# A two-layer hybrid decoder trunk on one core: two small experts in one slot, and the final norm inside the last slot

## The reference, cut to what matters

```python
def _rmsnorm(x, g):
    y = x * lax.rsqrt(jnp.mean(x * x, axis=-1, keepdims=True) + EPS)
    return y * g

def expert_block(xb, e):                       # D = D_FF = 1024
    hb = xb @ w1[e] + b1[e]                    # w1: 1024 x 2048
    x_glu = jnp.minimum(hb[:, :D_FF], 7.0)
    x_lin = jnp.clip(hb[:, D_FF:], -7.0, 7.0)
    return (x_glu * sigmoid(1.702 * x_glu) * (x_lin + 1.0)) @ w2[e] + b2[e]

h = h + sum over a token's 4 experts of gate * expert_block(norm(h), e)
out = _rmsnorm(h, norm_final)
```

## Time and profile before

| | us |
|---|---|
| median of three runs | 2594.08 |
| lowest and highest run | 2588.51 and 2594.45 |
| the profiled execution, its own time | 2597.89 |
| its span, from the first to the last instruction | 2596.1 |
| TensorE busy, all phases | 2418.1 |
| first expert matmul to last | 890.3 to 2551.5 |
| mean granted TensorE clock | 0.968 |

### The profile page before, as it was taken

One profiled execution on the slowest core, in us unless ns is written; L12 is line 12 of the kernel. 1 busy time (PEld: TensorE's weight loads), 2 busy tenths in 40 slices (PEclk: granted clock), 3 DMA queues, 4 the chain that ended last, 5 costly groups with the idle time before them and its releaser, 6 DMA issues. The chain is left out here.

```text
span 2596.1 us, 29106 instructions
## 1 busy us (share of the span) xinstructions
PE 2418.1 (93%) x11256; PEld 1585.8 (61%) x11257; DVE 632.6 (24%) x1536; ACT 365.9 (14%) x825; POOL 431.4 (17%) x998
## 2 busy tenths in 40 slices
PE   7899988989896699999999999999999999999993
PEld 3445556434443485968769678587686686684441
DVE  2031165222435521212122122121121221211111
ACT  3001054011311001010110101100101111101111
POOL 3806882020010101010000100000001001000002
PEclk9999988999997899999999999999999999999996
DMA  8604111610005558586787887878878888989854
GB/s 196 162 0 65 44 16 53 163 60 0 1 1 209 196 180 243 202 265 215 270 273 249 265 272 264 268 258 273 278 256 281 287 284 281 299 282 314 283 173 146
DMA packets 373344, 508.03 MB, mean 196 GB/s; under 512 B 49032, under 2 KB 234632, under 8 KB 373205
## 3 DMA queue, kind: packets, MB, share of 16 engines
q1 hardware_dynamic: 360872, 469.43, 55.0%
q0 software_dynamic: 11008, 35.89, 6.2%
q10 hardware_dynamic: 1324, 0.83, 0.1%
HBM read 469.39 MB, written 38.77 MB: 196 GB/s over the span
## 5 line engine op out<-in xcount | busy, mean ns | idle before, releaser
L2069 PE MATMUL ps<-xT,we 128*128 128x160 f32 (+9 forms) x3584 | 516.7, 307 | 1.4 <-ACT xT L2316 1.4
L2069 PEld LDWEIGHTS ps<-xT,we 128*128 128x128 f32 x3584 | 508.5, 190 | 15.1 <-issue 8.0
L2011 PE MATMUL ps<-we,xT 128*128 128x512 f32 x1152 | 506.8, 594 | 0.0
L2011 PEld LDWEIGHTS ps<-we,xT 128*128 128x128 f32 x1152 | 213.8, 190 | 258.5 <-issue 258.5
L2083 PE MATMUL ps<-actT,we 128*128 128x160 f32 (+9 forms) x1792 | 261.1, 307 | 0.0
L2083 PEld LDWEIGHTS ps<-actT,we 128*128 128x128 f32 x1792 | 253.4, 190 | 5.6 <-DVE outT L2230 2.1
L2035 PE MATMUL ps<-we,actT 128*128 128x512 f32 x576 | 255.1, 596 | 0.7 <-ACT actT L2347 0.7
L1906 POOL DMA_INDIRECT acc_dram<-orow,sx x46 | 70.9, 1542 | 779.0 <-ACT orow L2327 487.2
L2339 ACT ACTIVATE sg<-glu 128x512 f32<-128x512 f32 (+9 forms) x92 | 49.8, 541 | 1040.7 <-DVE glu L2185 549.6
L2035 PEld LDWEIGHTS ps<-we,actT 128*128 128x128 f32 x576 | 106.6, 190 | 135.1 <-issue 134.2
L795 PE MATMUL ps<-xnT,wa 128*128 128x512 f32 x384 | 168.9, 601 | 7.6 <-DMA wa<-in_w_in 7.6
(11 more groups left out here) (333 smaller groups left out, 2143.8 us busy)
## 6 DMA issues: line engine op xcount, KB each, us to landing
we<-in_w SPq DMA_DIRECT2D x384, 1024.0 KB, 5.9
wa<-in_w_in SPq DMA_DIRECT2D x4, 2048.0 KB, 12.9
xrow<-in_x SPq DMA_DIRECT2D x32, 128.0 KB, 7.4
wa<-in_w_xkv SPq DMA_DIRECT2D x2, 2048.0 KB, 10.2
h<-in_x SPq DMA_DIRECT2D x4, 1024.0 KB
acc_dram<-h SPq DMA_DIRECT2D x1, 4096.0 KB
fin<-acc_dram SPq DMA_DIRECT2D x8, 512.0 KB, 8.9
out<-fout SPq DMA_DIRECT2D x32, 128.0 KB, 2.4
```

What stands on the lines that cost most here:

```text
L2011: last = nc.tensor.matmul(m.ps[:, 2 * part + c, :], m.xT[:, 4 * half + k, 0:P], view[:, k, :], start=False, stop=(half == 1 and k == 3), s ...
L2069: last = nc.tensor.matmul(bank[:, part * WIN:part * WIN + W], view[:, k, (j % 2) * P:(j % 2 + 1) * P], m.xT[:, k, 0:W], start=(k == 0), st ...
```

## The change

The ranks 30 and 31 get a width of 64 and one slot for both, the second; there are 31 slots. A slot's pieces now come expert by expert in turn, so the joined slot has 24. Each of its matmuls is done twice, once for each expert: 64 columns of tokens stationary, PSUM partitions 0 to 63 for the one and 64 to 127 for the other, same bank. Its bias matmuls have three rows, with the rows that select the half in `sel`. It has two gathers and two scatters of 64 rows, the second scatter waiting for the first. Three VectorE instructions are added before the first slot.

The phase of the final norm is gone. In the last slot, once the scatter of the slot ahead has landed, SP loads four blocks, waits for them, and loads four more; POOL gathers the last slot's own rows from `acc_dram` into `tail`. ACT squares four blocks between the slot's two sigmoids and four after its last copy for the second layer. POOL makes the roots, VectorE scales in place, SP stores. VectorE then adds the last slot's result from PSUM to `tail`; ACT, POOL and VectorE norm it, and POOL stores it by index over the rows already stored. The last slot's own scatter is done only if tokens spilled, and then the whole norm is repeated.

The diff, cut to its core:

```diff
-RANK_WIDTH = (256, 224, 200, 168, 164, 164, 160, 160, 160, 156, 144, 136, 136, 132) + (P,) * 18
-RANK = tuple(r for i in range(14) for r in (i, 31 - i)) + (17, 16, 15, 14)
+RANK_WIDTH = (256, 224, 200, 168, 164, 164, 160, 160, 160, 156, 144, 136, 136, 132) + (P,) * 16 + (64, 64)
+SLOTS = ((0,), (30, 31)) + tuple((r,) for i in range(1, 14) for r in (i, 30 - i)) + ((16,), (15,), (14,))
...
 def piece_used(eng, n):
-        s, i = divmod(n, PIECES)
+        s = max(t for t in range(NS) if PIECE0[t] <= n)
+        i = (n - PIECE0[s]) // len(SLOTS[s])
...
     def _(sp):
...
+            if s == 0:
+                sp.dma_start(m.gfin[:], a.norm_final.rearrange("(a n) -> a n", a=1).to_broadcast([P, D])).then_inc(gfin_in, 16)
+                sp.dma_start(m.high[ST:P], m.gate_l[0:ST]).then_inc(high_in, 16)
+                for r in range(4):
+                    sp.dma_start(m.sel[32 * r:32 * r + 1, 0:ST], ...)
+                    sp.dma_start(m.sel[32 * r + 2:32 * r + 3, ST:P], ...)
+                for r in (2, 3):
+                    sp.dma_start(m.sel[32 * r + 1:32 * r + 2, :], ...)
...
+        q = out_tile(LAST - 1, 0)
+        sp.wait_ge(scattered[q % 2], 16 * (q // 2 + 1))
+        piece_used(sp, PIECE0[LAST] - 1)
+        for b in range(NB):
+            if b % 2 == 0 and b >= 4:
+                piece_used(sp, PIECE0[LAST] + b // 2 - 2)
+            sp.dma_start(m.fin[:, b], a.acc_dram[b * P:(b + 1) * P]).then_inc(block_in, 16)
+            if b == 3:
+                sp.wait_ge(block_in, 64)
+        for b in range(NB):
+            sp.wait_ge(block_ok, b + 1)
+            store(sp, b, block_out)
+        sp.wait_ge(block_out, 64 * NB)
+        sp.wait_ge(tail_out, 16)
...
     def _(pool):
...
+                if paired[s]:
+                    pool.indirect_dma_start(a.acc_dram, ... m.sx[0:ST, s % 3, 0:1] ..., orow[q % 2][0:ST, :], ...).then_inc(pair_out, 16)
+                    pool.wait_ge(pair_out, 16 * paired[:s + 1].count(True))
+                    pool.indirect_dma_start(a.acc_dram, ... m.sx[0:ST, s % 3, 1:2] ..., orow[q % 2][ST:P, :], ...)
...
-        scatter(E - 1)
-        for q in (tile0[E] - 1, tile0[E] - 2):
-            pool.wait_ge(scattered[q % 2], 16 * (q // 2 + 1))
+        before = out_tile(LAST - 1, 0)
+        pool.wait_ge(scattered[before % 2], 16 * (before // 2 + 1))
+        outputs_read(pool)
+        pool.indirect_dma_start(m.tail[:], None, a.acc_dram, ... m.sx[:, LAST % 3, 0:1] ...).then_inc(tail_in, 16)
+        ch = Chain(pool, root_step)
+        for b in range(NB):
+            pool.wait_ge(block_sq, b + 1)
+            root(nc, m, ch, b, D).then_inc(block_root, 1)
+        pool.wait_ge(tail_sq, 1)
+        root(nc, m, ch, NB, D).then_inc(tail_root, 1)
+        pool.wait_ge(block_out, 64 * NB)
+        pool.wait_ge(tail_idx, 4)
+        pool.wait_ge(tail_ok, 1)
+        pool.indirect_dma_start(a.out..., ... m.row_out[:, 2:3] ..., m.tail[:], ...).then_inc(tail_out, 16)
+        pool.wait_ge(tail_out, 16)
...
     def _(pe):
...
+        def rows_by_weights(s, i, bank, moved, half):
+            shared = len(SLOTS[s])
+            views = []
+            for x in range(shared):
+                piece_ready(s, shared * i + x)
+                views.append(piece_view(m, s, shared * i + x))
+            for k in range(4):
+                for x, view in enumerate(views):
+                    cols = slice(ST * x, ST * x + ST) if shared == 2 else slice(0, P)
+                    last = nc.tensor.matmul(m.ps[cols, bank, :], moved[:, 4 * half + k, cols], view[:, k, :], start=False,
+                                            stop=(half == 1 and k == 3), skip_group_check=True)
+            return last
...
     def _(dve):
         v.memset(m.outT[:], 0.0).then_inc(init_f, 1)
+        v.memset(m.sel[:], 0.0).then_inc(init_f, 1)
+        v.memset(m.high[:], 0.0).then_inc(init_f, 1)
+        v.tensor_scalar(m.low[:, 0:1], m.at_row[:, 0:1], float(ST), None, ALU.is_lt).then_inc(init_f, 1)
...
+        def scale(b, rooted, done):
+            dve.wait_ge(rooted, b + 1)
+            v.scalar_tensor_tensor(out=m.fin[:, b], in0=m.fin[:, b], scalar=m.rs[:, b:b + 1], in1=m.gfin[:], ...).then_inc(done, 1)
+        dve.wait_ge(gfin_in, 16)
+        for b in range(NB):
+            scale(b, block_root, block_ok)
...
+        link(v.tensor_tensor(c0, c0, c1, ALU.bitwise_or))
+        v.tensor_tensor(c2, c2, c0, ALU.bitwise_or).then_inc(tail_idx, 1)
+        dve.wait_ge(tail_in, 16)
+        for n in range(2):
+            dve.wait_ge(l2_full, l2_before[LAST] + n + 3)
+            v.scalar_tensor_tensor(out=out, in0=m.ps[:, 4 + n, :], scalar=m.gs[:, LAST % 3, 0:1], in1=out, ...).then_inc(tail_sum, 1)
+        dve.wait_ge(tail_root, 1)
+        v.scalar_tensor_tensor(out=m.tail[:], in0=m.tail[:], scalar=m.rs[:, NB:NB + 1], in1=m.gfin[:], ...).then_inc(tail_ok, 1)
...
     def _(act):
...
+        def square(b, loaded, count, done):
+            act.wait_ge(loaded, count)
+            if b:
+                act.wait_ge(done, b)
+            nc.scalar.activation(m.jf[:], m.fin[:, b], ACT.Square, accum_out=m.ss[:, b:b + 1]).then_inc(done, 1)
...
                 for c in range(2):
                     swish(s, c, P)
...
+                    if s == LAST and c == 0:
+                        for b in range(4):
+                            square(b, block_in, 64, block_sq)
                     if c == 1:
                         act_out(s, 0)
                 act_out(s, 1)
+                if s == LAST:
+                    for b in range(4, NB):
+                        square(b, block_in, 16 * NB, block_sq)
...
+        act.wait_ge(tail_sum, 2)
+        act.wait_ge(block_sq, NB)
+        nc.scalar.activation(m.jf[:], m.tail[:], ACT.Square, accum_out=m.ss[:, NB:NB + 1]).then_inc(tail_sq, 1)
+        narrow_rows(LAST)
...
-def phase_g(nc, block, m, a, sem):
...
-PHASES = [phase_abc, phase_d, phase_e, phase_f, phase_g]
+PHASES = [phase_abc, phase_d, phase_e, phase_f]
```

More of the change, by code:

```diff
@@ L1947, in _ @@
             pool.reg_mov(count, 0)
+            pool.sem_inc(spilled, 1)
+            once_more = Chain(pool, again["step"])
+            for b in range(NB):
+                pool.wait_ge(again["sq"], b + 1)
+                root(nc, m, once_more, b, D).then_inc(again["root"], 1)
         pool.reg_mov(flag, 0)
@@ L1996, in narrow @@
                 pe.wait_ge(l1_free, free_before[s])
-            loads = sum(1 for t in range(s) if not wide[t] and t % 2 == s % 2)
-            pe.wait_ge(row_in[s % 2], 16 * 6 * (loads + 1))
+            pe.wait_ge(row_in[s % 2], 16 * rows_in[s])
+            if paired[s]:
+                pe.wait_ge(high_in, 16 * 11)
             for r in range(4):
-                k = 2 if r >= 2 else 1
-                last = nc.tensor.matmul(m.ps[:, r, :], m.ones[32 * r:32 * r + k, :], m.brow[32 * r:32 * r + k, s % 2, :],
+                k = 3 if paired[s] else 2 if r >= 2 else 1
+                last = nc.tensor.matmul(m.ps[:, r, :], (m.sel if paired[s] else m.ones)[32 * r:32 * r + k, :], m.brow[32 * r:32 * r + k, s % 2, :],
                                         start=True, stop=False, skip_group_check=True)
@@ L2007, in narrow @@
                         i = 4 * c + 2 * part + half
-                        piece_ready(s, i)
-                        view = piece_view(m, s, i)
-                        for k in range(4):
-                            last = nc.tensor.matmul(m.ps[:, 2 * part + c, :], m.xT[:, 4 * half + k, 0:P], view[:, k, :], start=False,
-                                                    stop=(half == 1 and k == 3), skip_group_check=True)
+                        last = rows_by_weights(s, i, 2 * part + c, m.xT, half)
                         last.then_inc(l1_full, 1)
@@ L2031, in narrow @@
                     i = 8 + 2 * half + n
-                    piece_ready(s, i)
-                    view = piece_view(m, s, i)
-                    for k in range(4):
-                        last = nc.tensor.matmul(m.ps[:, 4 + n, :], m.actT[:, 4 * half + k, 0:P], view[:, k, :], start=False,
-                                                stop=(half == 1 and k == 3), skip_group_check=True)
-                    last.then_inc(l2_full, 1)
+                    rows_by_weights(s, i, 4 + n, m.actT, half).then_inc(l2_full, 1)
         def second_free(s):
@@ L2303, in _ @@
             dve.reg_mov(count, 0)
+            for b in range(NB):
+                scale(b, again["root"], again["ok"])
         dve.reg_mov(flag, 0)
```

248 lines of the change are left out of this document (150 added, 98 removed).

## The result

The kernel after the change takes 2526.07 us (median of 4 runs, 2524.50 to 2529.57), the one before 2594.06 beside it (4 runs, 2588.51 to 2594.45). The ratio is 0.9745, with an interval of 0.9728 to 0.9762: 68 us, or 2.6%, faster. The forecast was 2530.4.

A forecast was written before the change was run, and what follows sets the result against it. TensorE's matmul stream was taken to bound the expert slots, with the final norm uncovered behind them. Terms -45.9 + 1.5 + 0 + 0.7 - 20.0 = -63.7 gave 2534.2 profiled, 2530.4 us as median; range 2518 to 2546.

The forecast's parts named there:

- The joined slot, +1.5: Second slot: paired matmuls stream side by side as in a plain slot; array shape changes add 1.5 us, bounds 0 and 7.
- rival (b): Joined slot's matmul pairs overlap only in part; a quarter of the second stream exposed is +10 us, 2541; 6%.
- rival (a): Joined slot's pairs don't run side by side at 512 columns: 96 records more, +41 us, 2571.7; 4%.
- Weights, 0: Joined slot's 24 pieces: twelfth lands at 1016 or 1027, wanted at 1025.6 plus 1.5; no wait, bounds 0 and 7 us.
- Start, +0.7: Ahead of the first gather: three added VectorE instructions, covered by nothing, cost 0.7 us.
- ACT in the last slot: ACT waits for four blocks until about 2524, squares end at 2529; TensorE sees nothing, with 6 us to spare.
- Rival (e): Last slot: blocks land after 2531 and ACT holds up TensorE, some +5 us, 2535; 4%.
- From the last matmul to the store's issue, 9.2 us: End: remaining scaling, index instructions, sums, square, root and scaling run in line; indexed store some 9 us after the last matmul.
- The store's landing, 6.2: End: the indexed store takes 6.2 us from issue to landing, as for the last scatter.
- The drain, 7.6: End of block: POOL's DRAIN again follows an indexed DMA, so takes 7.6 us; bounds 0.35 and 7.6.
- rival (d): End of block: the last POOL drain is short, giving 2523 us; 10%.
- Rival (f): Joined slot: an expert exceeds 64 tokens, so the spill path and whole norm run again, +120 us, 2650; 2%.

The follow-up runs named there:

- experiment 1: Against the kernel after: every expert keeps its own slot (32 slots, no joined one), new start and end stay; 2568.27 us, ratio 0.9900 to the kernel before.
- experiment 2: Against the kernel after: both experts of the joined slot written to the same PSUM partitions, 0 to 63; 2570.84 us (one run).
- experiments 7 and 8: 7: kernel after without its last indexed store, 2522.36 us. 8: kernel after with last four squares earlier and an extra POOL drain in the last slot, 2516.67 us.
- Experiment 3: Against the kernel after: joined slot's matmul loops turned round, four of one expert then four of the other instead of in turn; 2540.09 us (one run).

## Why the prediction was right

The direction, the size and the account hold: 2526.07 lies in 2518 to 2546, 4.3 below the forecast. Against a sum of -63.7 the spans give -68.3; the two terms that were off, start and end, erred to the same side by 2.4 and 2.6 us. One of the prediction's own signs of being wrong did come: the time from the last matmul to the end is 22.0 us and not 24 to 25. By its steps:

- **One narrow slot less, -45.9.** Measured -45.94; experiment 1 gives 44.6 for the join as a whole, 45.94 less the extra below.
- **The joined slot, +1.5 for some twelve changes of shape.** Measured +1.20 in the second place and +1.09 in the 28th, 0.1 us per change in the mean. The far attention's pairs did carry over from 64 and 128 columns to 512: the pairs come every 0.43 us, which leaves nothing for rival (b), and experiment 2 shows what rival (a) would have looked like. That this rested on the order of the two experts inside the loop was not seen.
- **Weights, 0.** Right; the twelfth piece landed at 1020.3, between the 1016 and 1027 of the prediction.
- **Start, +0.7: wrong, with the wrong sign (-1.73).** The three VectorE instructions cost 0.43 at the gather, of the same order. The step that failed is the sentence that SP's twelve small loads go "ahead of loads that have slack": they do, but for that very reason they hold these loads back, and the gathers on which TensorE waits then don't share the DMA engines with 2 MB of weights. A queue that a step is moved past was looked at only for lateness.
- **ACT in the last slot.** The prediction had four blocks in by 2524 in the times of before, 18.1 us into the slot; the first square starts 17.3 us into it, the second sigmoid 22.8 (22.8 before), and the copy that TensorE needs isn't late. Rival (e) falls.
- **From the last matmul to the store's issue, 9.2 us.** Right: 2514.96 - 2505.80 = 9.16. The last scaling ended 2.6 us after the last matmul (3.0 predicted); a hop of 0.9 from VectorE's end to the issue, put at 0.1, was made up for by terms a little too large.
- **The store's landing, 6.2: mis-sized.** It landed 3.1 to 3.4 us after issue (2518.1 to 2518.4). The nearest row was the scatter that adds; this one only writes. These are the 2.8 us that the end was better than forecast; flag, branch and barriers took some 0.4 more than 1.4.
- **The drain, 7.6.** 7.67 measured, and rival (d) falls. The prediction took the value because an indexed DMA stands just ahead of it; experiments 7 and 8 show that this reason was wrong: the number held since the phase happens to issue 93 indexed DMAs instead of 92. Here the prediction was lucky.

Rival (f), the spill path, didn't run: no window of spilled tokens stands in the trace.

## What to carry to other kernels

Two small products can share the array's two column halves at almost no cost, also with long streams (1.2 us on a slot of 49.5 here), if the two are issued alternately, matmul by matmul. A closing stage that waits for nothing but one slot's rows belongs under that slot, and then every instruction of it that stands behind a late copy in ACT's queue should be asked whether it could stand ahead. If POOL has issued many indexed DMAs (92 cost 7.6 us here), drain it where it idles, not at the end.

## What the runs showed of the hardware that was not expected

- **POOL's drain costs by the number of indexed DMAs since the last one, not by their age.** 92 gave 7576, 7584 and 7577 ns (the kernel before, experiments 7 and 8), 93 gave 7666, one gave 132: about 82 ns each, if it is even between 1 and 92, where no run lies. It isn't all that a drain can wait for: two of POOL's drains in earlier phases took 349 and 2207 ns in the kernel after with no indexed DMA before them. What it is that is worked off, the profile doesn't show.
- **Matmuls of the two column halves start out of program order, here ahead of three records of the other half.** Experiment 3: four alone, twelve pairs, four alone. It is inferred from the starts and the 643 ns marks. Other distances were not tried.
- **An indexed store that only writes lands in 3.1 to 3.4 us, one that adds in 6.1 to 6.3**, both of some 128 rows. The last one of each kind ran with no other load or store under way (issued at 2552.5 before, 2515.0 after). Only the two kinds as they stand in these kernels were seen, and they also differ in the tensors they go to.
- **Two weight pieces issued beside the first gathers delay them**: 7.3 us to landing with them 1.3 us ahead, 5.7 with them 0.9 us behind the first one (the kernel before), 4.9 without.
- **A change of array shape** cost 0.1 us in the mean, as twelve in the joined slot cost 1.1 to 1.2. By the starts of the records the twelve aren't alike: where full-width transposes or matmuls meet the half-width pairs the next start comes some 0.09 us later than with one shape throughout, and the step after the change is 0.05 longer; next to the bias matmuls, which change the shape in a plain slot too, nothing is added. The Trainium skill, TensorEngine Tiling (Array Packing), Key Properties, says that a change of tiling mode drains the TensorE. The trace shows a delay at these changes, this small; whether it is a drain it doesn't show.
